# The first layer's input and shift in two parts: the pooling's projection runs from features without the shift

## The chip, the cores and the metric

The kernel runs on one core of a Trainium2 chip. The metric is the device time of one execution in microseconds, the median over the timed runs.

## The reference, cut to what matters

A network of four blocks works on 256 tokens of width 1024, in float32. The change lies at the head of the first block, whose mixer is a "hybrid":

```python
def modulation(c, w, b):
    return jnp.split(jax.nn.silu(c) @ w + b, 3, axis=-1)

def sandwich(x, mod, g_pre, g_post, fn):
    shift, scale, gate = mod
    h = rms_norm(x, g_pre) * (1.0 + scale[:, None]) + shift[:, None]
    return x + gate[:, None] * rms_norm(fn(h), g_post)

def mixer(h, j=j):
    u, qr, fr, vr, gr = jnp.split(h @ hyb_w_in[j], split_at, axis=-1)
    y = jnp.concatenate([pool_mixer(u, pool_w[j], pool_scale[j]),
                         hgrn2_mixer(qr, fr, vr, gr, lower_bounds[j], hgrn_out_norm[j])], axis=-1)
    return y @ hyb_w_out[j]

# in pool_mixer, for each window: mean over the window, less the token itself
        diffs.append(window_sum / count - uf[:, :, sl])
```

The shift is the same for every token. It adds one constant per column to u, and the window's mean less the token itself takes that constant out again. The other parts (q, f, v, g) need the shift.

## The kernel before, in words

All products are float32. Each weight tile of 128 x 1024 is split by ScalarE into a high part (WH, `hi_to`, L1502) and by VectorE into the rest (WL, `lo_to`, L2025), and a product is three matmuls: high by high, high by low, low by high (`mm3`, L657 to L659). The features are kept in the same two parts, `xh` and `xl` (the tile XHL). A "piece" is one such weight tile, half of a group of 256 output columns over 1024 inputs, and costs TensorE 24 matmuls. The plan of pieces starts with the hybrid: u (pieces 0 to 3), q (4 to 7), f (8 to 11), v (12 to 15), g (16 to 19), then hyb_w_out. SP loads a piece `n + 4` when VectorE has made the low part of piece `n` (four raw slots). Both `hi_to(n)` and `lo_to(n)` work strictly in order, and are called from inside ScalarE's and VectorE's own lists of work (`filled(u)` calls them with three pieces of look ahead).

Conditioning: the vectors shift, scale and gate of a block come from `ada_w`, 24 tiles of 128 x 1024 for a block, 8 for each vector. VectorE multiplies and adds each tile into an accumulator (`ada_step(x)`, L2018 for the first, L2022 for the others), TensorE sums over partitions (`ada_total`, L654, 8 products of one column, shown as 16 records), and VectorE adds the bias (`ada_end`). The order is scale of block 0 (x = 0 to 7), shift of block 0 (8 to 15), scale of block 1 (16 to 23), gate of block 0 (24 to 31), and so on. Four of the shift's tiles (12 to 15, `ADA_BY_PE`) are multiplied by TensorE instead, 8 products of one column each (16 records). After the first ones, the steps are tied to weight pieces: the dictionary in `ada_plan` names the piece behind whose low part each step runs on VectorE, and TensorE makes the total ahead of the piece behind the last one.

The order at the head, before the change:

- SP: some constants, x, the 16 tiles of conditioning in the order of `ADA_FIRST`, weight piece 0, the rest of constants and parameters (651 and 794 KB), pieces 1 to 3, `invc`, tiles 16 to 19, then the wait for the features' low parts (`s_xl`) ahead of `pool_w`, then the plan.
- TensorE: 14 warm-up products, tiles 12 and 13, the 16 transposes of x (`pre(0)`, 32 records, which need the diagonals made of the mean squares), tile 14, the total of the scale, tile 15, the total of the shift, the wait for the rest of the constants, u, q, f, the pooling's product `pp`, and then v and g with the eight "levels" of the recurrence between their pieces.
- ScalarE: the squares of x, high part of piece 0; with both vectors there, `keep_features` reads each transposed feature and writes scale times it plus shift to t2 (L1491).
- VectorE: tiles 0 to 3, the mean, the diagonals, tiles 4 to 11, ends of scale and shift, the low part of piece 0, `split_features(0)` (cast to xh, subtraction to xl), the bounds of the gates, copies of u out of PSUM, and then `lo_to` with the conditioning's steps and the five parts of `pooling` between them. In the levels it multiplies and masks between the pieces.

## Time and profile before

| what | value |
| --- | --- |
| timed runs | 1469.47, 1475.51, 1469.47 us; median 1469.47 us |
| profiled execution | 1477.99 us |
| its span | 1476.2 us, 23563 instructions |
| TensorE busy | 1419.5 us (96%) |
| VectorE busy | 1141.5 us (77%) |
| ScalarE busy | 819.6 us (56%) |
| mean granted clock of TensorE | 0.98 |
| transferred | 333.80 MB, mean 226 GB/s |

The profiled execution is one by itself: its span is the time from the first to the last instruction, and 1.8 us of its time lie around it. In the page and the views PE is TensorE, PEld its weight loads, DVE VectorE, ACT ScalarE, SPq the queue on which SP issues transfers. A float32 product shows as two records. "Idle before" is the time in which an engine had nothing to do ahead of an instruction, and the name behind it is that of what ended it.

### The profile page before, as it was taken

How to read it: one execution, taken by the hardware profiler on the slowest of the kernel's cores; microseconds unless marked ns; L12 is line 12 of the kernel's file. 1: busy time of each engine (PE TensorE's matmuls, PEld its weight loads, DVE VectorE, ACT ScalarE, POOL GpSimd, SP SyncE). 2: the span in 40 equal slices, each digit the busy share in tenths (PEclk: the TensorE clock that was granted, in tenths of full speed). 3: DMA queues.
4: the chain of work that ended last, by engine and by line, in shares of the span. 5: the costliest groups of instructions: out<-in, count | busy, mean ns of one | idle time of the engine just before them, and what ended most of it. 6: DMA issues, size and time to landing. Idle time of an engine off the chain costs nothing.

```text
span 1476.2 us, 23563 instructions
## 1 busy us (share of the span) xinstructions
PE 1419.5 (96%) x9034; PEld 1256.0 (85%) x9034; DVE 1141.5 (77%) x1824; ACT 819.6 (56%) x1196; POOL 2.0 (0%) x6
## 2 busy tenths in 40 slices
PE   7989899999999999999999999999999999899997
PEld 7888788888898979999989878888879998788886
DVE  4898787887865657787467657799988966879997
ACT  1442444544544446455465446788766564678874
POOL 0000000000000000000000000000000000000000
PEclk7899999999999999999999999999999999999999
DMA  9982389987575524655635224899953544589992
GB/s 366 326 297 104 125 299 348 341 327 268 166 236 170 186 72 142 197 178 185 188 114 172 87 97 165 299 391 375 377 179 115 160 127 157 181 318 391 373 364 84
DMA packets 184515, 333.80 MB, mean 226 GB/s; under 512 B 13372, under 2 KB 127828, under 8 KB 184404
## 3 DMA queue, kind: packets, MB, share of 16 engines
q1 hardware_dynamic: 184404, 332.31, 64.6%
q8 instruction: 72, 1.18, 0.3%
q14 instruction: 39, 0.32, 0.1%
HBM read 331.18 MB, written 1.09 MB: 225 GB/s over the span
## 4 chain that ended last, share of the span: by engine, by line
PE 77%; DVE 12%; DMA 5%; ACT 3%; issue 3%; SPq 0%; DVEq 0%; ACTq 0%
PE PSA L654 16%; PE PSA L657 13%; PE PSA L659 13%; PE PSA L658 13%; PE PSB L657 6%; PE PSB L658 6%; PE PSB L659 6%; PE PSB L654 4%; DVE WL L2025 2%; DVE ACC L2022 2%; DMA AD<-ada_w 2%; DMA WR<-ffn_w_in 1%; ACT WH L1502 1%; DVE T L2025 1%; DMA WR<-hyb_w_in 1%
## 5 line engine op out<-in xcount | busy, mean ns | idle before, releaser
L2025 DVE TENSOR_TENSOR WL<-WR,WH 128x1024 fp32r<-128x1024 f32 x352 | 422.3, 1219 | 108.4 <-ACT WH L1502 107.5
L1502 ACT CAST WH<-WR 128x1024 fp32r<-128x1024 f32 x352 | 357.3, 1048 | 114.0 <-DMA WR<-hyb_w_in 45.5
L657 PE MATMUL PSA<-XHL,WH 128*128 128x256 f32 x976 | 284.1, 291 | 7.8 <-ACT T L1491 2.2
L658 PE MATMUL PSA<-XHL,WH 128*128 128x256 f32 x976 | 278.0, 285 | 0.0
L659 PE MATMUL PSA<-XHL,WL 128*128 128x256 f32 x976 | 277.8, 285 | 0.0
L657 PEld LDWEIGHTS PSA<-XHL,WH 128*128 128x128 f32 x976 | 188.9, 194 | 13.5 <-issue 5.4
L658 PEld LDWEIGHTS PSA<-XHL,WH 128*128 128x128 f32 x976 | 189.1, 194 | 0.9 <-issue 0.5
L2025 DVE TENSOR_TENSOR WL<-AR,WH 128x1024 fp32r<-128x1024 f32 x152 | 178.3, 1218 | 14.1 <-ACT WH L1502 14.1
L659 PEld LDWEIGHTS PSA<-XHL,WL 128*128 128x128 f32 x976 | 188.9, 194 | 0.0
L657 PE MATMUL PSB<-WH,GH 128*128 128x512 f32 x400 | 158.8, 397 | 2.1 <-DVE GL L2025 2.1
L658 PE MATMUL PSB<-WL,GH 128*128 128x512 f32 x400 | 156.6, 392 | 0.0
L659 PE MATMUL PSB<-WH,GL 128*128 128x512 f32 x400 | 156.5, 391 | 0.0
L1502 ACT CAST WH<-AR 128x1024 fp32r<-128x1024 f32 x152 | 151.5, 1049 | 4.0 <-PE PSA L659 4.0
L654 PE MATMUL PSA<-XHL,WH 128*128 128x512 f32 x336 | 118.8, 397 | 2.1 <-ACT T L1491 1.7
L657 PE MATMUL PSA<-WH,XHL 128*128 128x256 f32 (+1 forms) x352 | 116.2, 330 | 3.9 <-DVE AR L2022 2.7
L659 PE MATMUL PSA<-WH,XHL 128*128 128x256 f32 (+1 forms) x352 | 113.5, 322 | 0.0
L658 PE MATMUL PSA<-WL,XHL 128*128 128x256 f32 (+1 forms) x352 | 113.3, 322 | 0.0
L654 PE MATMUL PSA<-XHL,WL 128*128 128x256 f32 x336 | 94.3, 281 | 0.0
L657 PEld LDWEIGHTS PSB<-WH,GH 128*128 128x128 f32 x400 | 75.6, 189 | 19.5 <-issue 4.4
L659 PEld LDWEIGHTS PSB<-WH,GL 128*128 128x128 f32 x400 | 75.5, 189 | 16.2
L658 PEld LDWEIGHTS PSB<-WL,GH 128*128 128x128 f32 x400 | 75.5, 189 | 15.3 <-issue 0.5
L1491 ACT ACTIVATE AR<-PSA 128x256 f32<-128x256 f32 (+1 forms) x71 | 31.2, 442 | 102.3 <-PE PSA L659 102.2
(290 smaller groups left out, 2354.3 us busy)
## 6 DMA issues: line engine op xcount, KB each, us to landing
AR<-moe_w_gate_up SPq DMA_DIRECT2D x96, 512.0 KB, 6.0
WR<-ffn_w_in SPq DMA_DIRECT2D x88, 512.0 KB, 4.7
WR<-moe_w_gate_up SPq DMA_DIRECT2D x64, 512.0 KB, 5.6
AR<-ada_w SPq DMA_DIRECT2D x59, 512.0 KB, 9.1
AR<-moe_w_down SPq DMA_DIRECT2D x56, 512.0 KB, 6.5
WR<-ffn_w_out SPq DMA_DIRECT2D x44, 512.0 KB, 4.3
WR<-att_w_qkv SPq DMA_DIRECT2D x36, 512.0 KB, 4.9
AD<-ada_w SPq DMA_DIRECT2D x34, 512.0 KB, 6.1
```

Source lines behind the costliest of these rows:

```text
L654: return e.matmul(o, l, r, start=start, stop=stop, skip_group_check=skip)
L657: e.matmul(o, lh, rh, start=start, stop=False, skip_group_check=True)
L658: e.matmul(o, lh, rl, start=False, stop=False, skip_group_check=True)
L659: return e.matmul(o, ll, rh, start=False, stop=stop, skip_group_check=True)
L1491: return e.activation(o, i, f, bias=bias, scale=scale)
L1502: A(e.copy(hi_slot(m), raw_slot(m)), s_hi)
L2022: return e.scalar_tensor_tensor(out=o, in0=i, scalar=s, in1=j, op0=op0, op1=op1)
L2025: return e.tensor_tensor(o, i, j, op)
```

## The change

Two more buffers are used as feature parts: `gh` and `gl` hold the features of block 0 without the shift, split by VectorE right behind ScalarE's `keep_features` with a bias of zero. The u pieces (0 to 3) are multiplied by these. The shifted features (`xh` by ScalarE from t2 with the shift as bias, `xl` by VectorE in one operation) come later, for q and all after it. TensorE's order becomes: warm-up, transposes, total of the scale, first u group, tiles 12 and 13, second u group, tiles 14 and 15, total of the shift, q. VectorE's becomes: tiles 0 to 3, diagonals, tiles 4 to 7, scale, low part of piece 0, the unshifted split with the low part of piece 1 in it, tile 8, low part of piece 2, tile 9, low part of piece 3, tiles 10 and 11, end of the shift, the shifted low parts. ScalarE takes over the copies of u. SP loads tiles 0 to 7 first, then four weight pieces and the shift's tiles in turn; the rest of the constants, `invc` and the tiles from 16 on are moved behind pieces of the plan, and so is the wait for `s_xl`. The steps 16 to 31 are tied to later pieces. Empty changes of the diff are left out below.

```diff
--- before.py
+++ after.py
@@ -173,7 +173,7 @@
             at = FIRST["ffn", 0] + 6
         if p == 10:
             at = FIRST["att"] + 2
-        pieces = {3: (12, 12, 13, 13, 16, 17, 17, 18), 4: (22, 22, 22, 22, 23, 24, 25, 26),
+        pieces = {2: (5, 5, 6, 7, 8, 9, 10, 11), 3: (15, 15, 16, 16, 17, 17, 18, 18), 4: (22, 22, 22, 22, 23, 24, 25, 26),
                   9: (82, 83, 84, 85, 86, 87, 88, 88)}.get(p, range(at, at + 8))
         for k in range(8):
             if 8 * p + k not in ADA_BEHIND_LEVELS:
@@ -193,7 +193,7 @@
 
 
 
-ADA_FIRST = (0, 1, 12, 2, 3, 4, 13, 5, 6, 7, 14, 8, 9, 15, 10, 11)
+ADA_FIRST = range(8)
 ADA_BY_PE = (12, 13, 14, 15)
 
 
@@ -227,7 +227,7 @@
         count.append(times[i])
         before.append(last.get(i))
         if x >= 20:
-            early = piece[x] - (9 if 24 <= x < 28 else 3 if 28 <= x < 32 else 8 if 32 <= x < 40 else 6)
+            early = piece[x] - (9 if 24 <= x < 28 else 3 if 28 <= x < 32 else 8 if 32 <= x < 40 else 4 if x < 24 else 6)
             if 22 <= i < 28:
                 early = max(early, FIRST["ffn", 0])
             load.setdefault(max(early, piece.get(before[x], 0)), []).append(x)
@@ -625,6 +625,7 @@
         s_glua, s_pad, s_conv, s_silu = (sig(f"s_{n}_made") for n in ("glua", "pad", "conv", "silu"))
         s_md, s_msb, s_mg, s_mh = (sig(f"s_{n}_made") for n in ("mdec", "msb", "mg", "mh"))
         s_open = sig("s_gates_open")
+        s_scale, s_xu, s_xhs = (sig(f"s_first_{n}") for n in ("scale", "unshifted", "shifted_high"))
         s_small, s_fsil, s_prod = (sig(f"s_ffn_{n}_made") for n in ("small", "silu", "product"))
         s_rd, s_ra = sig("s_route_dve"), sig("s_route_act")
         s_s5r = sig("s_s5_read")
@@ -697,13 +698,20 @@
             def half_of_features(u, half, stage):
                 n, h, l = piece()
                 h, l = v3(h, 4), v3(l, 4)
+                unshifted = n < 4
+                first = 4 if stage == "hyb" else FIRST[stage]
+                by_h, by_l = (gh, gl) if unshifted else (xh, xl)
                 for f in range(2):
                     for k in range(4):
                         kk = 4 * half + k
-                        if n - FIRST[stage] < 2 and f == 0:
+                        if n < 2 and f == 0:
+                            e.wait_ge(s_xu.sem, kk + 1)
+                        if first <= n < first + 2 and f == 0:
                             e.wait_ge(s_xl.sem, 8 * SPLIT[stage] + kk + 1)
                         t = mm3(bank(u.b, f * 256, f * 256 + 256), h[:, k, f * P:(f + 1) * P],
-                                l[:, k, f * P:(f + 1) * P], xh[:, kk, :], xl[:, kk, :],
+                                l[:, k, f * P:(f + 1) * P], by_h[:, kk, :], by_l[:, kk, :],
                                 half == f == k == 0, kk == 7)
                 t.then_inc(used(n)[0], 1)
 
@@ -912,24 +920,21 @@
             busy(14)
             shifts = use(("ada", 1), of=pring)
             e.wait_ge(s_csil.sem, 1)
-            for x in ADA_BY_PE:
-                if x == ADA_BY_PE[2]:
-                    pre(0)
-                if x == ADA_BY_PE[3]:
-                    ada_total(0)
-                e.wait_ge(s_ada[ADA_PLACE[x]].sem, 16 * ADA_COUNT[x])
-                for f in range(8):
-                    mm(bank(shifts.b, f, f + 1), ada_at[ADA_PLACE[x]][:, f * P:(f + 1) * P], csil[:, x - 8:x - 7],
-                       x == ADA_BY_PE[0] and f == 0, False, skip=True)
+            pre(0)
+            ada_total(0)
+            for s in range(2):
+                features(("u", s), "hyb")
+                for x in ADA_BY_PE[2 * s:2 * s + 2]:
+                    e.wait_ge(s_ada[ADA_PLACE[x]].sem, 16 * ADA_COUNT[x])
+                    for f in range(8):
+                        mm(bank(shifts.b, f, f + 1), ada_at[ADA_PLACE[x]][:, f * P:(f + 1) * P], csil[:, x - 8:x - 7],
+                           x == ADA_BY_PE[0] and f == 0, False, skip=True)
             e.wait_ge(s_adastep.sem, ada_count(15))
             for f in range(8):
                 t = mm(bank(shifts.b, f, f + 1), accs[1][:, f * P:(f + 1) * P], onesd[:, 0:1], False, f == 7, skip=True)
             t.then_inc(shifts.fill[0], 1)
 
 
-            e.wait_ge(s_rest.sem, 32)
-            for s in range(2):
-                features(("u", s), "hyb")
             for s in range(2):
                 features(("q", s), "hyb")
             for s in range(2):
@@ -943,6 +948,7 @@
                     t = mm(bank(u.b, x * 256, x * 256 + 256), poolw[:, g, :], dif[:, g, :], True, True)
                 t.then_inc(u.fill[0], 1)
             q4, k4 = v3(Qh, 4), v3(Kh, 4)
+            e.wait_ge(s_rest.sem, 32)
 
             def level(li):
                 e.wait_ge(s_lev.sem, li + 1)
@@ -1529,10 +1535,18 @@
                 shift, sc = MC[:, n * 24:n * 24 + 8], MC[:, n * 24 + 8:n * 24 + 16]
                 if n == 0:
                     hi_to(0)
-                e.wait_ge(*(ring if n else pring).uses["ada", ADA_PARTS.index((n, 0))].free)
+                    e.wait_ge(s_scale.sem, 1)
+                    for j in range(8):
+                        if j == 4:
+                            hi_to(1)
+                        keep_features(0, j, sc[:, j:j + 1], 0.0)
+                    hi_to(3)
+                    e.wait_ge(*pring.uses["ada", 1].free)
+                    for j in range(8):
+                        A(act(xh[:, j, :], t2[:, j, :], ACTF.Identity, bias=shift[:, j:j + 1]), s_xhs)
+                    return
+                e.wait_ge(*ring.uses["ada", ADA_PARTS.index((n, 0))].free)
                 for j in range(8):
-                    if n == 0 and j == 4:
-                        hi_to(1)
                     keep_features(n, j, sc[:, j:j + 1], shift[:, j:j + 1])
 
             def post(n, stage):
@@ -1597,7 +1611,11 @@
             pre(0)
 
 
-            e.wait_ge(s_rest.sem, 32)
+            for s in range(2):
+                u = ring.uses["u", s]
+                hi_to(4 + s)
+                e.wait_ge(*u.fill)
+                A.frees(e.copy(U[:, 2 * s:2 * s + 2, 16:272], v3(bank(u.b), 2)), u)
             for s in range(2):
                 u = ring.uses["q", s]
                 filled(u)
@@ -1607,6 +1625,7 @@
                 filled(u)
                 act(Fh[:, s * 512:(s + 1) * 512], bank(u.b), ACTF.Sigmoid)
                 A.frees(act(Kh[:, s * 512:(s + 1) * 512], bank(u.b), ACTF.Sigmoid, scale=-1.0), u)
+            e.wait_ge(s_rest.sem, 32)
             for s in range(2):
                 u = ring.uses["pp", s]
                 filled(u)
@@ -2084,7 +2103,7 @@
                 V.frees(tt(m, bank(u.b, 0, 8), par("adab", n * 24 + part * 8, 8), ALU.add), u)
                 if part == 1:
                     V.wait()
-                    V(stt(m, m, 1.0, par("npre", n * 8, 8), ALU.add, ALU.mult))
+                    V(stt(m, m, 1.0, par("npre", n * 8, 8), ALU.add, ALU.mult), None if n else s_scale)
 
             def rsqrt(v, y, t, sig=None):
 
@@ -2276,15 +2295,29 @@
             for x in range(4):
                 ada_step(x)
             diagonals(rms(st_pre, 4))
-            for x in range(4, 12):
+            for x in range(4, 8):
                 ada_step(x)
             ada_end(0)
+            lo_to(0)
+            for j in range(8):
+                if j == 4:
+                    lo_to(1)
+                e.wait_ge(s_t2.sem, j + 1)
+                V(e.tensor_copy(gh[:, j, :], t2[:, j, :]))
+                V.wait()
+                V(tt(gl[:, j, :], t2[:, j, :], gh[:, j, :].bitcast(F32), ALU.subtract), s_xu)
+            ada_step(8)
+            lo_to(2)
+            ada_step(9)
+            lo_to(3)
+            for x in (10, 11):
+                ada_step(x)
             ada_end(1)
-            lo_to(0)
-            split_features(0)
-            e.wait_ge(s_rest.sem, 32)
+            for j in range(8):
+                e.wait_ge(s_xhs.sem, j + 1)
+                V(stt(xl[:, j, :], t2[:, j, :], MC[:, j:j + 1], xh[:, j, :].bitcast(F32), ALU.add, ALU.subtract), s_xl)
             V(e.memset(U[:, :, 0:16], 0.0))
             e.wait_ge(s_ahyb.sem, 1)
             V(e.reciprocal(h_lb, h_e0))
@@ -2296,13 +2329,9 @@
             V(ts(h_lb, h_lb, 0.0, None, ALU.max))
             V.wait()
             V(ts(h_om, h_lb, -1.0, 1.0, ALU.mult, ALU.add))
-            for s in range(2):
-                u = ring.uses["u", s]
-                filled(u)
-                V.frees(e.tensor_copy(U[:, 2 * s:2 * s + 2, 16:272], v3(bank(u.b), 2)), u)
-            V.wait()
             def pooling():
+                for s in range(2):
+                    e.wait_ge(*ring.uses["u", s].free)
                 V.wait()
                 V(tt(w2[:, :, 1:272], U[:, :, 1:272], U[:, :, 0:271], ALU.add))
                 yield
@@ -2337,6 +2366,7 @@
             for _ in pool:
                 pass
             total = Fh
+            e.wait_ge(s_rest.sem, 32)
 
             def halves(h):
 
@@ -3074,16 +3104,11 @@
                 e.dma_start(XT[:, m * 1024:(m + 1) * 1024], a["x"][m * P:(m + 1) * P, :]).then_inc(s_x.sem, 16)
             for x in ADA_FIRST:
                 load_ada(x)
-            load_raw(0)
-            for t, name, n in ((CT, "consts", EARLY_CONSTS), (PR, "params", EARLY_PARAMS)):
-                e.dma_start(t[:, n:], a[name][:, n:]).then_inc(s_rest.sem, 16)
-            for n in range(1, NRAW):
-                load_raw(n)
-            e.dma_start(invc, a["aux"][:, 0:1024]).then_inc(s_invc.sem, 16)
-            for x in range(16, 20):
-                load_ada(x)
-            e.wait_ge(s_xl.sem, 8)
-            e.dma_start(poolw, a["pool_w"][0].rearrange("g c d -> c g d")).then_inc(s_poolw.sem, 16)
+            for x in ("r0", "r1", 8, 12, "r2", 9, 13, "r3", 10, 14, 11, 15):
+                if x in range(16):
+                    load_ada(x)
+                else:
+                    load_raw(int(x[1]))
             for n in range(len(PLAN)):
                 if n in rows_at:
                     load, k = rows_at[n]
@@ -3112,6 +3137,17 @@
                         e.dma_start(glu[k], a["s5_w_glu_2"][0][P * k:P * k + P, :]).then_inc(s_glu.sem, 16)
                 if n + NRAW < len(PLAN):
                     load_raw(n + NRAW)
+                if n < 3:
+                    load_ada(16 + n)
+                if n == 2:
+                    e.dma_start(invc, a["aux"][:, 0:1024]).then_inc(s_invc.sem, 16)
+                if n == 3:
+                    e.wait_ge(s_xl.sem, 8)
+                    e.dma_start(poolw, a["pool_w"][0].rearrange("g c d -> c g d")).then_inc(s_poolw.sem, 16)
+                    load_ada(19)
+                if n == 6:
+                    for t, name, c in ((CT, "consts", EARLY_CONSTS), (PR, "params", EARLY_PARAMS)):
+                        e.dma_start(t[:, c:], a[name][:, c:]).then_inc(s_rest.sem, 16)
                 for x in ADA_LOAD.get(n, ()):
                     load_ada(x)
             for b in range(4):
```

## Rows read from the trace of the kernel before

**Rows 1.** The page: busy time of the engines over the span.
```profile
PE 1419.5 (96%) x9034; PEld 1256.0 (85%) x9034; DVE 1141.5 (77%) x1824; ACT 819.6 (56%) x1196; POOL 2.0 (0%) x6
```

**Rows 2.** Stages (windows): busy time of each engine, PEclk, DMA share, GB/s.
```profile
15.00:25.00 10.00, 10.00 (x61) 9.97 (x60) 8.80 (x18) 0.00 (x0) 0.00 (x0) 0.66 1.03 410
25.00:37.30 12.30, 12.21 (x71) 12.13 (x70) 3.08 (x6) 1.04 (x1) 0.00 (x0) 0.62 1.06 381
...
54.20:80.60 26.40, 25.45 (x211) 25.00 (x210) 23.60 (x28) 14.81 (x16) 0.00 (x0) 1.00 0.97 321
80.60:104.00 23.40, 19.25 (x155) 18.63 (x154) 22.04 (x30) 8.85 (x14) 0.00 (x0) 0.98 0.77 275
104.00:129.00 25.00, 25.00 (x182) 24.02 (x183) 18.77 (x30) 6.38 (x7) 0.00 (x0) 0.88 0.62 241
```

**Rows 3.** Timeline of TensorE, 0 to 60: start, duration, operation.
```profile
15.21 4.64 PE L654 MATMUL PSB<-SM,AR 128*128 128x1 f32 x32
...
33.66 3.55 PE L654 MATMUL PSB<-CT,AR 128*128 128x1 f32 x16
39.43 0.55 PE L657 MATMUL PSA<-XHL,WH 128*128 128x256 f32 x1 [2.22 <-ACT T L1491]
...
44.65 0.40 PE L659 MATMUL PSA<-XHL,WL 128*128 128x256 f32 x1
```

**Rows 4.** Short stages (windows), columns as in rows 2.
```profile
18.00:19.00 1.00, 1.00 (x6) 1.00 (x6) 0.89 (x2) 0.00 (x0) 0.00 (x0) 0.50 1.02 406
24.00:25.00 1.00, 1.00 (x9) 1.00 (x9) 1.00 (x1) 0.00 (x0) 0.00 (x0) 0.79 1.03 414
28.00:30.00 2.00, 2.00 (x11) 2.00 (x11) 1.83 (x2) 0.00 (x0) 0.00 (x0) 0.50 1.05 414
44.00:45.00 1.00, 1.00 (x6) 0.77 (x4) 0.97 (x3) 0.04 (x1) 0.00 (x0) 0.55 0.69 111
```

**Rows 5.** Timeline of VectorE, 0 to 90.
```profile
15.01 0.15 DVE L2022 SCALAR_TENSOR_TENSOR MC<-MC 128x2 f32<-128x2 f32 x1
...
17.17 5.45 DVE L2022 SCALAR_TENSOR_TENSOR ACC<-AR,SM,ACC 128x1024 f32<-128x1024 f32 x4
...
30.85 0.17 DVE L2022 SCALAR_TENSOR_TENSOR MC<-MC,PR 128x8 f32<-128x8 f32 x1
37.25 0.17 DVE L2025 TENSOR_TENSOR MC<-PSB,PR 128x8 f32<-128x8 f32 x1 [6.23 <-PE PSB L654]
...
42.64 0.75 DVE L2025 TENSOR_TENSOR XHL<-T,XHL 128x256 fp32r<-128x256 f32 x2
43.36 0.11 DVE L2288 MEMSET AR<- 128x64 f32 x1
```

**Rows 6.** Timeline of ScalarE, 0 to 90.
```profile
37.45 1.94 ACT L1491 ACTIVATE T<-PSA,MC 128x256 f32<-128x256 f32 x4 [5.63 <-DVE MC L2025]
```

**Rows 7.** Timeline of VectorE, 86 to 180.
```profile
113.30 1.43 DVE L2025 TENSOR_TENSOR AR<-AR 128x512 f32<-128x512 f32 x3 [1.73 <-PE PSA L654]
```

**Rows 8.** Timeline of TensorE in the q, f and level stages.
```profile
70.17 1.84 PE L654 MATMUL PSA<-CT,ACC 128*128 128x1 f32 x16
...
95.73 2.05 PE L654 MATMUL PSA<-AR 128*128 128x128 f32 x16 [1.07 <-DVE AR L2025]
...
103.73 3.79 PE L654 MATMUL PSB<-AR 128*128 128x128 f32 x16 [3.09 <-DVE AR L2025]
```

**Rows 9.** Groups of VectorE's instructions by line, 44 to 87: busy, mean ns, idle.
```profile
L2025 DVE TENSOR_TENSOR WL<-WR,WH 128x1024 fp32r<-128x1024 f32 x13 | 15.9, 1220 | 3.0 <-ACT WH L1502 2.9
...
L2025 DVE TENSOR_TENSOR AR<-AR 128x256 f32<-128x256 f32 (+4 forms) x9 | 6.1, 703 | 0.2
...
L2302 DVE COPY AR<-PSA 128x512 f32<-128x512 f32 x2 | 1.4, 684 | 0.0
```

**Rows 10.** Waits of SP's queue and of ScalarE, 0 to 120: total, times, longest.
```profile
SPq L3046 <- DVE XHL L2025: 9.1, 1, 9.1
...
ACT WH L1502 <- DMA WR<-hyb_w_in: 45.5, 11, 20.9
```

## The prediction, made before the changed kernel was run

> **What bounds the kernel now.** I read the page first. TensorE is busy for 96% of the span [rows 1], so the kernel's time is TensorE's own work plus the few stretches in which TensorE waits or runs at half clock. Next I read the opening in stages [rows 2]. From 15 to 37.3 us TensorE is busy, but at a clock of 0.66 and 0.62, and the transfers fill the DMA engines. From 54.2 to 80.6 us TensorE is nearly full at full clock. From 80.6 to 104 us it loses 4.15 us (23.40 less 19.25) while VectorE is busy for 22.04 of 23.40. After 104 us it is full again.
>
> TensorE's order of work [rows 3] shows what the opening is made of. Behind the warm-up come the two blocks 12 and 13 (32 records of one column, from 15.21), the 32 transpose records, block 14 (16 records), the total of the scale (16), block 15 (16) and the total of the shift (16), up to 37.21. The first feature product starts at 39.43. VectorE, in order [rows 5], multiplies the pieces as they land, has the scale at 31.02 and the shift at 37.42, and goes on with the splits. In the stage of levels, VectorE is the one that is late: TensorE waits 1.07 and 3.09 us for it, at 95.73 and 103.73 [rows 8]. Later VectorE waits for TensorE (1.73 us at 113.30) [rows 7]. So up to level 3 VectorE's list is the path, and from there TensorE's is.
>
> **The clock.** Where one-column products follow dense ones, the clock falls: it is 0.50 in 18 to 19, some 3 us into the one-column blocks, with TensorE shown busy in all of it; it rises during the transposes (0.79 in 24 to 25), is at 0.50 again in 28 to 30, and rises 5 us after the dense feature products started (0.55 in 44 to 45) [rows 3, 4]. At full clock a one-column record costs 1.84 / 16 = 0.115 us [rows 8], at half clock 3.55 / 16 = 0.22; a feature piece (24 matmuls) takes 5.15 us at half clock (39.43 to 44.65, 0.213 each [rows 3]). At full clock it takes 2.9 (0.12 each: the last 24 of the piece from 67.22 are done at 70.17 [rows 8]).
>
> **The change, part by part.**
>
> 1. Transfers. The scale's pieces 0 to 7 land without pieces 12, 13 between them. Two transfers fewer lie ahead of piece 7, and one ahead of piece 3. A transfer of 512 KB takes 1.28 us at 410 GB/s [rows 2]. Before, the first four steps end at 15.0 [rows 5]; one landing earlier is 13.7. Mean and diagonals take 17.17 − 15.01 = 2.2, four steps 5.45 (17.17 to 22.62): the scale's steps end at 21.3 instead of 22.6. That is only 1.3 us, because VectorE and no longer the DMA sets it.
>
> 2. TensorE's transposes wait only for the diagonals (15.9) and no longer for blocks 12 and 13 (15.21 + 4.64 = 19.85 [rows 3]). They run at full clock, 16 records of this size in 2.05 or less [rows 8], so they end near 19.8. The scale's total starts at 21.3 and, partly at half clock, takes about 2.8 (between 1.84 and 3.55): 24.1. Two small operations give the scale at 24.6 (31.02 before). ScalarE's first feature follows 0.5 later, VectorE splits the first piece of weights (1.2) and casts and subtracts (I take 0.6 for a feature: the subtractions start 0.33 apart [rows 5], 0.2 for the cast, and the subtraction now waits for its own cast): the first product starts at about 26.6. It was 39.43, so the start is 12.8 us earlier.
>
> 3. What stood ahead of 39.43 has not gone. Blocks 12 and 13, 14 and 15 and the shift's total are now behind the two u groups. In TensorE's order: first half of u0 at half clock 5.15, to 31.7; second half at full, 34.6; blocks 12 and 13, begun at full and ended at half clock, 4.6 (4.48 before), to 39.2; u1 at half, then full clock, 5.15 + 2.9, to 47.2; blocks 14 and 15, 4.6, to 51.8; the total at half clock 3.55, to 55.4. Call this T. Every landing is earlier: block 15, the last of 16 pieces, is there by about 33. With the clock full throughout T would be 48.7 (26.6, u0 to 33.7 by VectorE's pace: eight features and one piece of weights, 25.9 + 4.8 + 1.2 = 31.9, and the 13 to 15 matmuls behind it, 1.8; then 32 × 0.115, 5.8, 32 × 0.115, 1.8); with it at half throughout 64.8 (4 × 5.15, 64 × 0.22, 3.5).
>
> The Trainium skill ("TensorE: Matmul & The Clock Gate", section "HAM oscillation — how this bites in real kernels") describes a clock lost through gaps, while matmuls wait for data. By that rule alone my three changes of clock within T, where TensorE has no gap, would not come, and the time would be that of the rival with T near 48.7. The rows of before differ: the clock is 0.50 from 18 to 24 us with TensorE busy throughout [rows 4].
>
> 4. The new wait. VectorE's list runs steps 8 to 11 and the weight pieces 2 and 3 until about 39, and then stands at the shift's total, until T: some 16 us. Everything behind stands too, above all the low part of weight piece 4, which TensorE needs for q0. In before this wait was 6.2 us [rows 5]. ScalarE waits at the same place: eight shifted copies take 3.9 (four take 1.94 [rows 6]), VectorE follows each with one subtraction (0.4 behind the last), then come the bounds of the gates (0.85 for seven small operations from 43.36 on [rows 5]), then the low part of piece 4 (1.2). The 0.2 of the shift included, VectorE resumes at T + 5.4 = 60.8, and q0 can start at T + 6.6 = 62.0. Before, the fifth piece started at 54.2 by the count of four pieces behind 39.43.
>
> 5. VectorE then paces q and f. Up to piece 11's low part it does 8 low parts (1.14 start to start, 1.22 long [rows 9]), steps 16 to 22 of the conditioning (0.67 + 6 × 1.2) and the pooling's nine operations (6.1 busy, 6.4 with gaps [rows 9]): 9.1 + 7.9 + 6.4 = 23.4, to 84.2. The two copies of U (1.4 [rows 9]) go to ScalarE, which is 56% busy in this stage [rows 2], and weigh nothing. TensorE ends piece 11 at 84.3 + 2.9 = 87.2, not at 80.6: +6.6. The low clock with which q0 starts (5.15 instead of 2.9) is hidden by this pace. The total of steps 16 to 23 (1.7 us of 16 records, at 70.17 before [rows 8]) moves from the middle of f0 to ahead of v0. There it is no longer in the stretch that I counted: +1.7, so level 0 is 8.3 late.
>
> 6. Levels 0 to 3. Steps 24 to 27 were done at weight pieces 12 and 13, that is before level 0 came due. Now they are behind pieces 15 and 16, between levels 0 and 1, where VectorE is the later one: 0.67 + 3 × 1.2 = 4.3, plus 0.4 for the end of the scale of the second layer, less step 28, which moves out (1.2): +3.5. Steps at piece 17 stay two in number. Piece 18 has one more, 1.2, which lies in the 1.73 us that VectorE waits for TensorE at 113.30 [rows 7]. Level 3 starts 11.8 late.
>
> 7. SP's queue. Behind n = 3 it waits for all shifted low parts (T + 4.6 = 60). Before, this wait cost it 9.1 us [rows 10]. Behind it are the pooling's weights, piece 19 of the conditioning, then weight piece 8. Four weight pieces (4 to 7) are already in, and VectorE comes to piece 8 at about 74: it lands by 64, at 1.3 us for 512 KB and several transfers. The late constants and parameters (1.44 MB, 4 us at the same rate) follow piece 10 and are needed at level 1, past 95. So the queue costs nothing, although it stands for some 15 us; if it were late it would show as ScalarE waiting for piece 11, and cost up to 3. The early queue saves nothing behind T: the waits of before on landings (3.0 us on VectorE through ScalarE's high parts [rows 9]) are not part of the new sum, since I built it from work alone.
>
> **Sum.** −12.8 at the first product; + 20.6 from there to q0 (35.4 instead of 14.8), which is +7.8; −1.2 over q and f, where the waits on landings fall away, +1.7 and +3.5: +11.8 us. From level 3 TensorE is 96 to 100% busy and nothing there changes, so I let all of it reach the end. The profiled execution has 1477.99 (span 1476.2 and 1.8 around it), the three timed runs 1469.47, 1469.47 and 1475.51; the difference is taken on the median, 1469.5 + 11.8 = **1481.3 us**. A measurement of this kernel tells about 0.5% (7.3 us) from no change.
>
> **Rivals.** A: the clock holds through the one-column work (the part that follows dense u0 and u1 at full clock). T is 48.7, and the time 6.7 lower: 1474.6. For it: the 16 such records at 70.17 ran at full clock [rows 8]. Against it: it fell each time thereafter.
> B: the clock is low more of the time, because q and f come in bursts at VectorE's pace and u0 is begun cold. T 60 to 64.8: 1486 to 1490.7. For it: behind the 3.09 us gap at 103.73 some 6 us ran at half clock (0.88 over 25 us [rows 2, 8]).
> C, the other side: landings, not VectorE's list, set the levels. ScalarE waited 45.5 us for weights of hyb_w_in in the first 120 us, in 11 waits [rows 10]. If the high part of pieces 17 and 18 had been what level 3 waited for, the earlier four weight pieces and the later conditioning would carry it, and the delay would end there: 1469.5 or a little less. It decides if VectorE has over 11.8 us of idle time before level 3. Against it: VectorE is busy for 22.04 of 23.40 there, and had 3.0 us of such waits from 44 to 87 [rows 2, 9].
> D: the early start pays in full. No change in time needs q0 11.8 earlier than 62.0, so T at 43.6, and even at full clock it is 48.7. It could only come with C.
>
> **Chances.** Forecast 0.62; A 0.13; B 0.12; C with D 0.13. Range: 1472 to 1491; A and B are inside, of C only its upper edge. Faster by over 0.5% (under 1462.1) 0.06; within 0.5% (to 1476.8) 0.20, most of A and C; slower 0.74.
>
> **What would show each step.** First product with GH at 26 to 28 us; the wait of VectorE for the shift's total at some 16 us from 39, ended at T = 52 to 57; first product with XHL at 60 to 64; clock 0.50 in part of 36 to 44 and again near 50 to 60; TensorE's waits in 55 to 85 for VectorE's low parts; level 0 at 93 to 96; SP standing for s_xl until about 60, with no wait of ScalarE for weights behind it. I am wrong if T is under 50, if TensorE is busy with q0 within 3 us of T, or if the stretch behind level 3 becomes shorter.

## The result, and the profile after

The changed kernel takes 1489.31 us (median of 4 runs, 1485.21 to 1492.19), the kernel before, in runs beside it, 1471.87 (4 runs, 1469.47 to 1475.51). The ratio is 1.012 with a 95% interval of 1.0096 to 1.0144, that is 14.1 to 21.2 us more. The forecast was 11.8 us more, 1481.3 us, in a range of 1472 to 1491. The profiled execution is the one of 1492.19 us. Its page begins with the span and the busy time of the engines over it:

```profile
span 1490.4 us, 23580 instructions
...
PE 1419.4 (95%) x9034; PEld 1254.3 (84%) x9034; DVE 1143.8 (77%) x1830; ACT 823.1 (55%) x1206; POOL 2.0 (0%) x6
```

TensorE's busy time is that of before [rows 1] within 0.1 us. So the difference of the spans, 1490.4 less 1476.2 = 14.2 us, is time in which TensorE is idle. Nearly all of it is lost early: the last masking operation of the levels (level 7) starts at 143.82 us on VectorE instead of 130.21, which is 13.6 of the 14.2.

The timeline of TensorE to 130 us, after (start, duration, operation; compare [rows 3]):

```profile
25.38 0.55 PE L658 MATMUL PSA<-GH,WH 128*128 128x256 f32 x1 [2.35 <-DVE GL L2044]
...
33.87 3.63 PE L655 MATMUL PSB<-SM,AR 128*128 128x1 f32 x32
...
44.67 1.84 PE L655 MATMUL PSB<-SM,AR 128*128 128x1 f32 x16
46.38 1.93 PE L655 MATMUL PSB<-SM,T 128*128 128x1 f32 x16
48.16 3.27 PE L655 MATMUL PSB<-CT,AR 128*128 128x1 f32 x16
57.63 0.55 PE L658 MATMUL PSA<-XHL,WH 128*128 128x256 f32 x1 [6.19 <-DVE WL L2044]
```

The first feature product is at 25.38, 1.2 us ahead of the forecast (26.6) and 14 us earlier than before. Blocks 12 and 13 come at 33.87, blocks 14 and 15 at 44.67 and 46.38, the shift's total at 48.16. Behind it TensorE stands for 6.19 us, until VectorE has made the low part of piece 4: q0 starts at 57.63 (54.2 before, forecast 62.0).

VectorE to 140 us, after (compare [rows 5]; the number in brackets is the idle time ahead of the operation and what ended it):

```profile
51.47 0.17 DVE L2044 TENSOR_TENSOR MC<-PSB,PR 128x8 f32<-128x8 f32 x1 [13.76 <-PE PSB L655]
52.22 3.27 DVE L2041 SCALAR_TENSOR_TENSOR XHL<-T,MC,XHL 128x256 fp32r<-128x256 f32 x8 [0.57 <-ACT XHL L1497]
...
79.65 1.23 DVE L2044 TENSOR_TENSOR WL<-WR,WH 128x1024 fp32r<-128x1024 f32 x1 [0.65 <-ACT WH L1508]
...
88.93 1.22 DVE L2044 TENSOR_TENSOR WL<-WR,WH 128x1024 fp32r<-128x1024 f32 x1
97.84 1.23 DVE L2044 TENSOR_TENSOR AR<-AR 128x1024 f32<-128x1024 f32 x1 [7.69 <-PE PSA L655]
...
110.53 1.32 DVE L2404 COPY_PREDICATED AR<-CT,PSB 128x512 f32<-128x512 int32 x2
```

VectorE stands 13.76 us at the shift (6.23 before). The shift itself comes at 51.47, and in the kernel before it came at 37.25. In the same timeline of before, VectorE's product behind level 0 starts at 87.23 and the first mask of level 1 at 96.19; here they are at 97.84 and 110.53. In the table, q0 is the first product of piece 4, the first one that uses the shifted features.

| from ... to | before | after | difference |
| --- | --- | --- | --- |
| start to the shift | 37.25 | 51.47 | +14.2 |
| shift to q0 | 17.0 | 6.2 | −10.8 |
| q0 to the end of f (the pooling's product starts) | 26.4 | 26.6 | +0.2 |
| end of f to VectorE's product behind level 0 | 6.6 | 13.6 | +6.9 |
| level 0 to the first mask of level 1 | 9.0 | 12.7 | +3.7 |
| that to the last mask of level 7 | 34.0 | 33.3 | −0.7 |
| sum | 130.2 | 143.8 | +13.6 |

The 10.8 us are u, which no longer lies behind the shift (four pieces, 14.8 before), less what the chain from the shift to the first product with it grew by (6.2 instead of 2.2, in which TensorE has nothing else to do). They are gone again by level 1. The piece of TensorE's timeline in which the 6.9 us are lost, after:

```profile
84.26 1.89 PE L655 MATMUL PSA<-AR,T 128*128 128x256 f32 x8
88.01 2.24 PE L655 MATMUL PSA<-CT,ACC 128*128 128x1 f32 x16 [1.86 <-ACT AR L1497]
...
95.37 2.38 PE L655 MATMUL PSA<-AR 128*128 128x128 f32 x16
...
110.06 2.29 PE L655 MATMUL PSA<-AR 128*128 128x128 f32 x9 [4.78 <-DVE AR L2044]
```

And the windows there and ahead of the shift, after (columns as in [rows 2]; the seventh value behind the span of time is the granted clock):

```profile
34.00:38.00 4.00, 4.00 (x38) 4.00 (x37) 3.61 (x4) 0.00 (x0) 0.00 (x0) 1.00 1.05 377
38.00:42.00 4.00, 4.00 (x23) 4.00 (x22) 0.00 (x0) 0.00 (x0) 0.00 (x0) 0.57 1.05 378
42.00:48.00 6.00, 6.00 (x55) 6.00 (x53) 0.00 (x0) 0.00 (x0) 0.00 (x0) 1.00 0.30 103
88.00:92.00 4.00, 3.99 (x25) 4.00 (x26) 2.15 (x5) 3.18 (x6) 0.00 (x0) 0.68 0.83 261
92.00:96.00 4.00, 4.00 (x20) 4.00 (x20) 0.00 (x0) 1.04 (x1) 0.00 (x0) 0.50 0.31 105
```

ScalarE, after:

```profile
51.67 3.30 ACT L1497 ACTIVATE XHL<-T,MC 128x256 fp32r<-128x256 f32 x8 [22.35 <-DVE MC L2044]
...
78.57 1.05 ACT L1508 CAST WH<-WR 128x1024 fp32r<-128x1024 f32 x1 [6.58 <-DMA WR<-hyb_w_in]
81.40 1.05 ACT L1508 CAST WH<-WR 128x1024 fp32r<-128x1024 f32 x1 [1.79 <-DMA WR<-hyb_w_in]
...
86.64 1.08 ACT L1497 ACTIVATE AR<-PSA 128x512 f32<-128x512 f32 x2
```

ScalarE stands 6.58 us for the landing of weight piece 11 and 1.79 for piece 12. Its sigmoids for f are behind these casts in its list; the second pair runs at 86.64 to 87.7. TensorE waits for it 1.86 us ahead of the total at 88.01. Behind this wait, in the one-column total, the clock falls (0.68 in 88 to 92, 0.50 in 92 to 96): the piece of v behind it takes 5.2 us instead of 2.9, and level 0 2.38 instead of 1.95. With the total itself (2.24), which stands here now (before at 70.17 [rows 8]), that is the 6.9: 1.9 + 2.3 + 0.4 + 2.2. SP's queue of transfers, after, in the view of waits (queue line, for whom, total, times, longest; compare [rows 10]):

```profile
SPq L3146 <- DVE XHL L2041: 16.5, 1, 16.5
```

### The profile page after: what moved, and what is told of

Read it like the earlier page. It is cut to its first block, busy times and chain, and to the rows that moved or that the text cites. A ratio compares the mean times of both kernels' runs of the same rounds, so it can differ in the third digit from the quotient of the medians.

```text
span 1490.4 us, 23580 instructions
## 1 busy us (share of the span) xinstructions
PE 1419.4 (95%) x9034; PEld 1254.3 (84%) x9034; DVE 1143.8 (77%) x1830; ACT 823.1 (55%) x1206; POOL 2.0 (0%) x6
## 4 chain that ended last, share of the span: by engine, by line
PE 73%; DVE 14%; DMA 5%; ACT 4%; issue 3%; SPq 0%; DVEq 0%; ACTq 0%
PE PSA L658 13%; PE PSA L660 13%; PE PSA L659 13%; PE PSA L655 12%; PE PSB L658 5%; PE PSB L660 5%; PE PSB L659 5%; PE PSB L655 4%; DVE WL L2044 3%; DVE ACC L2041 3%; DMA WR<-ffn_w_in 2%; DMA AD<-ada_w 1%; ACT WH L1508 1%; DVE AR L2044 1%; DVE T L2044 1%
## 5 line engine op out<-in xcount | busy, mean ns | idle before, releaser
L658 PE MATMUL PSA<-XHL,WH 128*128 128x256 f32 x944 | 274.7, 291 | 11.2 <-DVE WL L2044 7.3
L659 PE MATMUL PSA<-XHL,WH 128*128 128x256 f32 x944 | 269.1, 285 | 0.0
L660 PE MATMUL PSA<-XHL,WL 128*128 128x256 f32 x944 | 268.9, 285 | 0.0
L658 PEld LDWEIGHTS PSA<-XHL,WH 128*128 128x128 f32 x944 | 183.0, 194 | 16.2 <-issue 9.3
L659 PEld LDWEIGHTS PSA<-XHL,WH 128*128 128x128 f32 x944 | 183.2, 194 | 0.9 <-issue 0.5
L660 PEld LDWEIGHTS PSA<-XHL,WL 128*128 128x128 f32 x944 | 183.0, 194 | 0.0
L655 PE MATMUL PSA<-XHL,WL 128*128 128x256 f32 x336 | 94.2, 280 | 0.0
```

What stands on the lines that cost most here:

```text
L655: return e.matmul(o, l, r, start=start, stop=stop, skip_group_check=skip)
L658: e.matmul(o, lh, rh, start=start, stop=False, skip_group_check=True)
L659: e.matmul(o, lh, rl, start=False, stop=False, skip_group_check=True)
L660: return e.matmul(o, ll, rh, start=False, stop=stop, skip_group_check=True)
```

## The experiments

Each kernel was timed 5 to 12 times. The column "ratio" is to the kernel before, in runs beside it. The last three columns are read from the trace of one execution each: when VectorE has the shift, when it starts the product behind level 0, and how long the last mask of level 7 starts behind the shift. The last one is the better measure where kernels differ by 2 to 5 us, because the shift's own time moves by up to 1.8 us between executions in which the engines' work ahead of it is the same (51.47 in the changed kernel, 53.25 and 53.19 in the experiments on constants and on steps). About 0.6 us of that is a later first product (25.94 and 25.96 instead of 25.38), the rest the clock: blocks 12 and 13 took 3.63 us in the first of these and 4.9 in the others, in which it fell earlier. The last column moves with the clock too. Behind the shift e4, e5 and e11 leave everything as in the changed kernel, and show 90.6, 92.1 and 90.7 against its 92.4. So a gain behind the shift is known to some 2 us.

| kernel | us | ratio [95%] | shift | level 0 | shift to level 7 |
| --- | --- | --- | --- | --- | --- |
| before | 1470 to 1472 | 1 | 37.25 | 87.23 | 93.0 |
| changed | 1489.31 | 1.0120 [1.0096, 1.0144] | 51.47 | 97.84 | 92.4 |
| e1_fill | 1485.56 | 1.0103 [1.0085, 1.0121] | 52.99 | 95.11 | 88.1 |
| e2_early_consts | 1485.83 | 1.0106 [1.0087, 1.0124] | 53.25 | 94.52 | 87.3 |
| e3_steps_back | 1485.41 | 1.0104 [1.0078, 1.0129] | 53.19 | 99.19 | 86.9 |
| e5_interleave | 1486.67 | 1.0113 [1.0094, 1.0131] | 49.70 | 94.24 | 92.1 |
| e4_no_14_15 | 1481.67 | 1.0065 [1.0051, 1.0078] | 47.92 | 92.56 | 90.6 |
| e11_14_15_on_vector | 1484.19 | 1.0086 [1.0067, 1.0105] | 47.01 | 91.67 | 90.7 |
| e7_shift_before_u1 | 1482.45 | 1.0084 [1.0061, 1.0106] | 44.67 | 90.06 | 93.0 |
| e6_all | 1479.5 | 1.0053 [1.0040, 1.0066] | 48.92 | 93.66 | 85.6 |
| e8_all_and_order | 1475.45 | 1.0026 [1.0010, 1.0042] | 47.15 | 88.83 | 83.4 |
| e10_best | 1472.81 | 1.0012 [1.0001, 1.0024] | 44.09 | 87.92 | 85.6 |
| e9_before_steps_later | 1478.25 | 1.0043 [1.0028, 1.0059] | 37.11 | 86.00 | 96.4 |

**e1_fill.** VectorE and ScalarE use their wait for the shift.

```diff
-                    hi_to(3)
+                    hi_to(6)
                     e.wait_ge(*pring.uses["ada", 1].free)
...
             for x in (10, 11):
                 ada_step(x)
+            lo_to(6)
             ada_end(1)
```

> Theory (the wait of VectorE and ScalarE for the shift costs): the low parts of pieces 4 to 6 and conditioning steps 16 to 18 move from behind the shift into VectorE's 13.8 us wait, and ScalarE makes their high parts there. q0 starts about 1.2 us earlier (at about 56.4 instead of 57.6 in the trace) and then runs without the pace of VectorE; the list of VectorE is 7 us shorter behind the shift. If VectorE's list alone sets the end of f, f ends 5 to 7 us earlier and the kernel takes about 1483 to 1484. Rival (landings: SP stands until the shifted low parts are made, and the late constants lie ahead of piece 11): piece 11 is cast at 78 us as before, f ends where it did, and the kernel takes 1488 to 1489, no change.

By time it is between the two readings, 0.0017 of the ratio under the changed kernel, with intervals that overlap. By the trace q0 starts 1.4 us behind the shift instead of 6.2, and the levels end 4.3 us earlier behind the shift. But in q and f VectorE now meets landings (the arrival of transfers). Its timeline in this kernel, and below it TensorE's:

```profile
52.99 0.17 DVE L2044 TENSOR_TENSOR MC<-PSB,PR 128x8 f32<-128x8 f32 x1 [7.37 <-PE PSB L655]
...
61.89 1.28 DVE L2041 SCALAR_TENSOR_TENSOR ACC<-AR,SM,ACC 128x1024 f32<-128x1024 f32 x1 [2.24 <-DMA AR<-ada_w]
...
74.90 1.29 DVE L2041 SCALAR_TENSOR_TENSOR ACC<-T,SM,ACC 128x1024 f32<-128x1024 f32 x1 [2.26 <-DMA T<-ada_w]
...
80.03 1.23 DVE L2044 TENSOR_TENSOR WL<-WR,WH 128x1024 fp32r<-128x1024 f32 x1 [2.37 <-ACT WH L1508]
```

```profile
81.31 0.58 PE L658 MATMUL PSA<-XHL,WH 128*128 128x256 f32 x1 [4.36 <-DVE WL L2044]
...
86.60 1.94 PE L655 MATMUL PSA<-AR,T 128*128 128x256 f32 x8
88.37 1.87 PE L655 MATMUL PSA<-CT,ACC 128*128 128x1 f32 x16
```

Of the 7 us that were taken out, 2.24 + 2.26 + 2.37 come back as waits for conditioning tiles and for piece 11. TensorE waits 4.36 us for the low part of piece 11 and does that piece at half clock, so that f ends 33.6 us behind the shift (86.60 less 52.99), and not earlier than in the changed kernel (32.8). What is won shows between the end of f and level 0: 8.5 us instead of 13.6, without TensorE's wait ahead of the total. So filling the wait brought q0 forward, but by the end of f the landings, and the half clock behind them, had taken it all. How much of the 4.3 us is due to the filled wait, and how much to the place at which the clock fell, is not shown.

**e2_early_consts.** The late constants and parameters go out ahead of SP's stand.

```diff
-                if n == 6:
+                if n == 2:
                     for t, name, c in ((CT, "consts", EARLY_CONSTS), (PR, "params", EARLY_PARAMS)):
                         e.dma_start(t[:, c:], a[name][:, c:]).then_inc(s_rest.sem, 16)
```

> Only the order of transfers changes: the rest of the constants and parameters (1.44 MB) goes out behind piece 6, ahead of SP's stand for the shifted low parts, where the DMA engines are idle from about 45.5 to 55.5. Rival to my prediction's 'the queue costs nothing': piece 11 is cast some 4 us earlier than 78.57, ScalarE is not late for the f group, TensorE does not idle 1.9 us ahead of v0, the clock stays full there, and level 0 is done 3 to 7 us earlier: the kernel takes 1483 to 1486. By the prediction (VectorE's list alone) VectorE has idle time of about 3 us to lose there: 1486 to 1489.

TensorE in this kernel, end of f to level 0:

```profile
86.04 1.89 PE L655 MATMUL PSA<-AR,T 128*128 128x256 f32 x8
87.77 1.90 PE L655 MATMUL PSA<-CT,ACC 128*128 128x1 f32 x16
...
92.47 1.95 PE L655 MATMUL PSA<-AR 128*128 128x128 f32 x16
```

The wait of 1.86 us ahead of the total is gone, the total takes 1.90 us and level 0 1.95, and a piece of v (24 products) lies between 89.53 and 92.47: the clock is full. The end of f is 32.8 us behind the shift (86.04 less 53.25) as in the changed kernel (84.26 less 51.47). All of the 5.1 us that the levels end earlier are won between the end of f and level 0. This shows the order of transfers as a cause, and that its price was paid not at the landing but behind it: ScalarE's sigmoids late, TensorE idle, and half clock behind that. The size is less certain. Four more kernels keep the late order, and in each TensorE waits 1.6 to 1.7 us ahead of this total. From the end of f to level 0 they take 11.8 us (e5), 11.9 (e4 and e11) and 10.3 (e7, where the granted clock is 1.00 from 83 to 98 us), against 13.6 in the changed kernel and 8.5 here. So 1.9 us of the gain are there even where the clock held, and the rest depends on when it fell. The time (1485.83) agrees with the rival, but is not separated from the changed kernel's by itself.

**e3_steps_back.** Conditioning steps 24 to 27 back ahead of level 0 (for which 20 to 23 must be done by piece 8).

```diff
-        pieces = {2: (5, 5, 6, 7, 8, 9, 10, 11), 3: (15, 15, 16, 16, 17, 17, 18, 18),
+        pieces = {2: (5, 5, 6, 7, 7, 8, 8, 8), 3: (12, 12, 13, 13, 16, 17, 17, 18),
```

> Only the places of the conditioning steps change: steps 24 to 27 go back to pieces 12 and 13, where VectorE waits 7.7 us for level 0, and so that their accumulator is free, steps 20 to 23 go to pieces 7 and 8. The term of the prediction (steps between level 0 and level 1 cost 3.7 us) gives about 1485.6. Against it: steps 20 to 23 earlier delay the low parts of q and f by up to 3 us, which gives 1487 to 1489; and if landings or TensorE set the levels, nothing changes (1489).

VectorE's product behind level 0 and the first mask of level 1 in this kernel:

```profile
99.19 1.23 DVE L2044 TENSOR_TENSOR AR<-AR 128x1024 f32<-128x1024 f32 x1 [0.34 <-PE PSA L655]
...
108.15 1.34 DVE L2404 COPY_PREDICATED AR<-CT,PSB 128x512 f32<-128x512 int32 x2
```

They are 8.96 us apart, as before (87.23 to 96.19), against 12.69 in the changed kernel: the term of 3.5 in the prediction is 3.7. Level 0 comes 46.0 us behind the shift, 0.4 earlier than in the changed kernel, where VectorE had stood 7.69 us ahead of it; against e4, e5 and e11 (44.5 to 44.7) it is 1.4 later. So the steps cost between nothing and 1.4 us ahead of level 0. The time, 1485.41, is the 1485.6 that was expected, but by itself is not separated from the changed kernel's.

**e9_before_steps_later.** The same part the other way round: the kernel before, with the conditioning steps placed as in the change and nothing else.

```diff
-        pieces = {3: (12, 12, 13, 13, 16, 17, 17, 18),
+        pieces = {2: (5, 5, 6, 7, 8, 9, 10, 11), 3: (15, 15, 16, 16, 17, 17, 18, 18),
...
-            early = piece[x] - (9 if 24 <= x < 28 else 3 if 28 <= x < 32 else 8 if 32 <= x < 40 else 6)
+            early = piece[x] - (9 if 24 <= x < 28 else 3 if 28 <= x < 32 else 8 if 32 <= x < 40 else 4 if x < 24 else 6)
```

> The kernel before, with one part of the change alone: the conditioning steps 16 to 31 stand at the later weight pieces. In the changed kernel this part made level 0 to level 1 3.7 us longer (12.7 instead of 9.0 between VectorE's two products). The theory of VectorE's list gives the same here: steps 16 to 19 leave the time before q (VectorE waits there 2.5 us for landings and loses nothing), steps 24 to 27 come between level 0 and 1, and the time is 3 to 4 us over the kernel before: 1475 to 1476. If the levels had slack for it, 1472.

```profile
86.00 1.23 DVE L2025 TENSOR_TENSOR AR<-AR 128x1024 f32<-128x1024 f32 x1 [4.39 <-PE PSA L654]
...
98.69 1.33 DVE L2374 COPY_PREDICATED AR<-CT,PSB 128x512 f32<-128x512 int32 x2
```

By itself this part makes the kernel before slower by 0.43% (0.28 to 0.59%, 4 to 9 us). In the trace (VectorE, above) it waits 4.39 us ahead of level 0 and then takes 12.69 to the mask of level 1; the levels end 3.3 us later (133.55 against 130.21). Of all parts of the change it is the one whose loss is shown by time alone. The median, 1478.25, is 2 us over the expected 1475 to 1476, and its distance to the kernel before, 7.8 us, is over twice what the trace shows at the levels.

**e5_interleave.** One block of one-column products behind each piece of u.

```diff
-                features(("u", s), "hyb")
+                u = use(("u", s), fill=used(taken[0] + 1))
+                u.piece = taken[0] + 1
                 for x in ADA_BY_PE[2 * s:2 * s + 2]:
+                    half_of_features(u, x % 2, "hyb")
                     e.wait_ge(s_ada[ADA_PLACE[x]].sem, 16 * ADA_COUNT[x])
```

> TensorE alternates one piece of u with one block of one-column products instead of two pieces with two blocks; nothing else changes. Theory of the clock (it falls some 2.4 us into one-column work and comes back 4 to 5 us into dense work): a block of 1.84 us at full clock is short enough, the clock rises once and stays, and the shift is there 2.5 to 3 us earlier (48.5 instead of 51.4): 1486 to 1487. Rival: the clock goes by the mean of the work and is low in all of the mixed stretch: the shift 3 to 8 us later, 1492 to 1497.

The windows of this kernel, columns as in [rows 2]:

```profile
30.00:34.00 4.00, 4.00 (x37) 4.00 (x36) 3.90 (x9) 0.26 (x1) 0.00 (x0) 1.00 1.04 395
34.00:38.00 4.00, 4.00 (x37) 4.00 (x36) 3.90 (x4) 0.00 (x0) 0.00 (x0) 1.00 1.06 381
38.00:42.00 4.00, 4.00 (x37) 4.00 (x37) 0.66 (x1) 0.00 (x0) 0.00 (x0) 1.00 1.02 305
42.00:46.00 4.00, 4.00 (x36) 4.00 (x36) 0.00 (x0) 0.00 (x0) 0.00 (x0) 1.00 0.69 258
```

The clock rises once and is full until the shift's total. The changed kernel has 0.56 to 0.59 in 38 to 42. The shift comes at 49.70, 1.8 us earlier than there and 3.5 earlier than in e2 and e3, but later than the 48.5 that was expected; the length behind the shift stays (92.1). The gain in time, 0.0007 of the ratio, is inside the noise.

**e4_no_14_15** leaves out the products of the shift's blocks 14 and 15, two of its eight blocks; **e11_14_15_on_vector** computes them as steps on VectorE, in its wait.

```diff
 # e4
                 for x in ADA_BY_PE[2 * s:2 * s + 2]:
                     e.wait_ge(s_ada[ADA_PLACE[x]].sem, 16 * ADA_COUNT[x])
+                    if s:
+                        continue
 # e11
-ADA_BY_PE = (12, 13, 14, 15)
+ADA_BY_PE = (12, 13)
...
-            for x in (10, 11):
+            for x in (10, 11, 14, 15):
                 ada_step(x)
             ada_end(1)
```

> The products of the shift's blocks 14 and 15 on TensorE are left out (so the shift lacks two eighths of its sum); their transfers stay. It asks whether time taken off ahead of the shift reaches the end one for one. They take 3.8 us in the changed kernel's trace (44.67 to 48.31), so the shift is there at 47 to 49. If everything hangs on the shift (VectorE, ScalarE and SP all stand for it), the end of the levels is as far behind the shift as before (92 us) and the time is 3 to 4 us lower: 1485 to 1486. If something else holds the levels (landings behind a queue that starts at a fixed time), the gain is under 1 us: 1488 to 1489.

> Blocks 14 and 15 of the shift are done by VectorE as steps (2.5 us in its wait of 13.8) instead of by TensorE (3.8 us at full clock); the order is else that of the changed kernel. The shift comes at 47 to 49 and all that stands for it moves along, as where the two blocks were left out: 1482 to 1485. If VectorE were on the path to the shift, nothing or a loss: 1489 or more.

The shift comes 3.6 and 4.5 us earlier and the levels end 5.3 and 6.2 earlier. Both are more than one for one; the rest lies at level 0, where the granted clock from 84 to 98 us is 0.88 and not 0.76. It is 0.88 in e5 too, which leaves out no block, so that part is not due to these edits. The ratios are lower by 0.0055 (intervals apart) and 0.0034 (intervals that overlap); e4, at 1481.67, is faster than either reading of its expectation. So time ahead of the shift does reach the end, and VectorE had room for the two blocks.

**e7_shift_before_u1.** TensorE's order alone: the shift's total stands ahead of the second u group.

```diff
-            for s in range(2):
-                features(("u", s), "hyb")
...
+            half_of_features(u, 0, "hyb")
+            block(12)
+            half_of_features(u, 1, "hyb")
+            for x in (13, 14, 15):
+                block(x)
+            e.wait_ge(s_adastep.sem, ada_count(15))
...
+            features(("u", 1), "hyb")
```

> TensorE's order alone: first half of u0, block 12, second half of u0, blocks 13, 14, 15, total of the shift, and only then u1. Theory: the 6.2 us from the shift to q0 (shifted copies, low parts, gates' bounds, low part of piece 4) now lie beside u1, and the shift comes at 44 to 47 instead of 51.5: q0 at 52 to 54 instead of 57.6, and all behind it 4 to 6 us earlier: 1483 to 1485. Rival (the clock: five one-column groups in a row run at half clock and u1 starts at half clock): the shift at 49 or later, q0 at 56 or later, and 1487 or more.

The shift comes at 44.67, q0 at 52.49. The levels end 6.2 us earlier (137.65 against 143.82), all of it ahead of the shift, since u1 is now behind it and covers the chain there. The time, 1482.45, is just below the range expected by the theory (1483 to 1485).

**e6_all** joins e1, e2, e3 and e5; **e8_all_and_order** joins e1, e2, e3 and e7.

```diff
 # e6: the edits of e1, e2, e3 and e5 above
 # e8: the edits of e1, e2, e3 and e7 above
```

> The four edits together (VectorE fills its wait, constants ahead of SP's stand, conditioning steps 24 to 27 back ahead of level 0, blocks one at a time). If the terms are separate ones, their gains against the end of the levels add up: 4.3, 5.1 and 5.5 us behind the shift and 2 to 3 in it. VectorE's list and the landings are two sides of one stretch, so I expect the first two to give about 6 together, and in all 11 to 13: 1476 to 1478. If they all remove the same wait: 1482 to 1484.

> The first three edits and the order in which the shift's total stands ahead of u1. Then q0 starts at about 53 with TensorE as the only limit to the end of f: piece 11 ends near 78 (80.6 in the kernel before), level 0 is done at 85 (87.2 before), and the levels keep their length: 1469 to 1472, no slower than the kernel before. If the clock takes it back, or the levels are held by VectorE's list as before, 1474 to 1478.

e6 takes 1479.5 us, 1.5 over the range for separate terms and below that for one shared wait: most of them are separate. Where it misses, VectorE stands for a conditioning tile that its new place asks for too early, and TensorE 5.8 us for VectorE:

```profile
71.00 1.28 DVE L2043 SCALAR_TENSOR_TENSOR ACC<-AR,SM,ACC 128x1024 f32<-128x1024 f32 x1 [5.43 <-DMA AR<-ada_w]
```

e8 takes 1475.45, in the range of its rival. TensorE is almost always busy to the end of f there, but in the stretch in which blocks 13, 14, 15 and the total follow each other, and u1 behind them, mostly at half clock (0.59):

```profile
36.00:50.00 14.00, 14.00 (x79) 14.00 (x78) 10.67 (x15) 5.78 (x10) 0.00 (x0) 0.59 0.85 316
```

**e10_best.** What the others point to: blocks 14 and 15 on VectorE, the order u0 first half, 12, u0 second half, 13, u1 first half, total, u1 second half; piece 4's low part ahead of the shift; e2; steps 20 to 23 at pieces 8 and 9, 24 to 27 at 13.

```diff
-ADA_BY_PE = (12, 13, 14, 15)
+ADA_BY_PE = (12, 13)
...
-        pieces = {2: (5, 5, 6, 7, 8, 9, 10, 11), 3: (15, 15, 16, 16, 17, 17, 18, 18),
+        pieces = {2: (5, 5, 6, 7, 8, 8, 9, 9), 3: (13, 13, 13, 13, 16, 17, 17, 18),
...
-                    hi_to(3)
+                    hi_to(5)
...
-            for x in (10, 11):
+            for x in (10, 11, 14, 15):
                 ada_step(x)
+            lo_to(4)
             ada_end(1)
...
-                if n == 6:
+                if n == 2:
```

> What the runs point to: blocks 14 and 15 on VectorE, TensorE's order u0 first half, block 12, u0 second half, block 13, u1 first half, total of the shift, u1 second half; weight piece 4 made ahead of the shift; constants ahead of SP's stand; steps 20 to 23 at pieces 8 and 9, 24 to 27 at 13. The one-column groups are short, so the clock stays full, the shift is there at 42 to 45 and q0 starts at 46 to 49 (54.2 in the kernel before). If TensorE is then the limit, level 0 is 4 to 6 us earlier than before and the time 1466 to 1469. Rival: VectorE's list (24 us of work from 47 on) or landings behind SP's stand take over in q and f, and it ends within 2 us of the kernel before: 1470 to 1474.

VectorE's timeline of this kernel, and below it, from the view of waits, TensorE's waits for low parts (total, times, longest):

```profile
44.09 0.17 DVE L2052 TENSOR_TENSOR MC<-PSB,PR 128x8 f32<-128x8 f32 x1 [0.90 <-PE PSB L655]
...
80.56 0.41 DVE L2046 TENSOR_SCALAR AR<-AR,SM 128x256 f32<-128x256 f32 x1 [4.99 <-ACT AR L1505]
...
87.92 1.23 DVE L2052 TENSOR_TENSOR AR<-AR 128x1024 f32<-128x1024 f32 x1
```

```profile
PE PSA L658 <- DVE WL L2052: 5.1, 7, 2.0
```

q0 starts at 46.87, 7.3 us before that of the kernel before, and level 0 is 0.7 us later than there. TensorE waits 5.1 us in 7 places for VectorE's low parts, 4.7 of them in q and f, where there are conditioning steps and the pooling between them. f ends at 79.24, only 1.4 us before that of the kernel before. VectorE then stands 4.99 us for f's last sigmoids, and has steps 24 to 27 behind them, so that it comes to level 0 2.1 us after TensorE's product (83.84 to 85.79). So the start that the unshifted u makes possible is used up by VectorE's list before level 0. The time, 1472.81, is 0.12% over the kernel before (0.01 to 0.24%), the range of the rival and not of the theory; none of these versions beats it.

One remainder runs through all of them. The distance of the medians is larger than the distance at the last mask (130.21 in the kernel before) by 1.5 to 6.3 us in each of the twelve kernels, 3.8 in the changed one and 2.9 in e10, whose levels even end 0.6 us earlier. All twelve are compared with the same single trace of the kernel before, of an execution slower than all its timed ones. So either its levels usually end some us earlier than in that trace, or something behind the levels costs as much; no run separates the two.

## Why the prediction was right, and where it was off

The direction, and the mechanism named first, were right: everything but u hangs on the shift, the change puts it later, and VectorE, ScalarE and SP stand in their lists until it is there.

1. and 2. The scale and the early start: forecast 26.6 for the first product, measured 25.38. Right.
3. T, the time of the shift: forecast 55.4, measured 51.4 (53.2 in other executions). Mis-sized by 2 to 4 us. I let the clock fall behind every group of one-column products. Measured, it fell once between the start of u and the total; blocks 14 and 15 ran at full clock and took 3.5 us (44.67 to 48.16), not 4.6, and blocks 12 and 13 took 3.5 (to 37.36), not 4.6 (in e1 to e4 they did take 4.9). The first product was 1.2 earlier than forecast, too. e5 shows that a block of 1.84 us between pieces leaves the clock full throughout, and e8 what four groups in a row cost. Rival A, the clock that holds, was half right. The Trainium skill ("TensorE: Matmul & The Clock Gate", "HAM oscillation — how this bites in real kernels") has the clock lost while TensorE waits for data. The piece of v at half clock does follow a wait, of 1.86 us, but that is shorter than the waits in the section's example, and behind the same wait in e7 (1.68 us) the clock held; nor does the rule cover 38 to 42 us, where TensorE was busy for 4.00 of 4.00 and the granted clock was 0.56 and 0.59.
4. The wait: forecast 16 us for VectorE, measured 13.76; q0 6.6 us behind T, measured 6.2 (57.63 less 51.4). Right.
5. VectorE's pace: forecast 25.2 us from q0 to the end of f, measured 26.6. VectorE paced TensorE only up to piece 9, whose first product (75.52) is the last to wait for a low part; the last three pieces ran at TensorE's own 2.9 us each, to 84.26. The forecast had VectorE's whole list and one piece behind it. The queue is not the reason: e2 has the same 26.6.
6. Steps 24 to 27 between levels 0 and 1: forecast +3.5, measured +3.7, and shown from both sides (e3, e9). Right.
7. The step that failed: "the queue costs nothing". Its term was put at 0, with 3 as the worst case. Piece 11 was cast at 78.57, when the pieces before it had been cast by 68.25, and the cost came behind that, as 1.86 us of wait and half clock in v and level 0. e2 puts its worth at 5.1 us against the changed kernel's trace, and at 1.9 to 3.4 against e4, e5, e7 and e11. Of the signs that the prediction named, two failed with it: ScalarE did wait for weights behind SP's stand, and level 0 came at 97.84, not at 93 to 96. I had followed the landings only to VectorE's low part, and not to ScalarE's sigmoids, which stand behind the same casts.

Against the forecast of 11.8 the trace has 4.0 less for T, 0.4 less from T to q0, 1.4 more in q and f, 5.2 more between the end of f and level 0 (6.9 less the 1.7 that was forecast), 0.2 more at level 1 and 0.7 less behind it: 13.5, against the 13.6 at the end of the levels. Two errors of similar size and opposite sign hid each other in the forecast, so that its closeness to the trace is in part luck. The medians are 17.4 apart, with an interval that reaches from 14.1 to 21.2. What the traces account for (14.2) lies at its lower edge. The remaining 3 us go the same way as the remainder of the experiments, and their cause stays open. Rival C, landings instead of VectorE's list, fell as a way to a faster kernel; landings did matter, but to the loss.

## What to carry to other kernels

When a value is taken off the path for one consumer, work out when it comes for all the others: here four pieces of u were freed from the shift, and the shift came 14.2 us later for everything else. An engine that works through its list in order makes each wait for the new, later value a wait for all that is behind it, so put independent work ahead of the wait or beside it (e7 and e11; e1 gained too, though the landings took part of it), and do that for the transfer queue as well (e2). Follow a late landing past its first reader to every operation that stands behind that reader in the same list.
